# A hybrid decoder layer on one core: two slices of the last gated chunk's projection are multiplied between the first attention scores

## The reference

```
h = rmsnorm(x, norm_g)
proj = einsum('bsd,de->bse', h, w_in)
y_lru = rglru_group(u, z, ...)   # width-4 convolution, gated linear recurrence, times silu(z)
y_nsa = nsa_group(...)           # 8 heads: compressed + selected + window branch, gated, times silu(z)
y_fox = fox_group(...)           # 8 heads: causal softmax with cumulative log forget gates, times silu(z)
return x + einsum('bse,ed->bsd', concat([y_lru, y_nsa, y_fox]), w_out)
```

## Time and profile before

| | |
|---|---|
| median of the runs | 422.81 us (422.7, 422.81, 423.13) |
| the profiled execution: its time, its span | 422.76 us, 421.0 us |
| TensorE matmuls busy | 413.4 us, 98% of the span |
| VectorE, ScalarE, GpSimd busy | 285.8, 261.0, 62.5 us |
| DMA moved | 40.51 MB |
| first attention, score 0 to score 16 | 136.61 to 148.57 us |

### The profile page before, as it was taken

One profiled execution on the slowest core, in us unless ns is written; L12 is line 12 of the kernel. 1 busy time (PEld: TensorE's weight loads), 2 busy tenths in 40 slices (PEclk: granted clock), 3 DMA queues, 4 the chain that ended last, 5 costly groups with the idle time before them and its releaser, 6 DMA issues.

```text
span 421.0 us, 6567 instructions
## 1 busy us (share of the span) xinstructions
PE 413.4 (98%) x2234; PEld 325.3 (77%) x2234; DVE 285.8 (68%) x616; ACT 261.0 (62%) x519; POOL 62.5 (15%) x122
## 2 busy tenths in 40 slices
PE   8999999999999899999999999999899999999996
PEld 7876788779888766666677987988676688888885
DVE  4667749988998966776368756699777489422205
ACT  5846996687465887886087778771887554322200
POOL 3000000000000666564000000000466100000000
PEclk9999999999999999999999999999999999999999
DMA  8913534421313000000322323439410315732005
GB/s 281 360 63 101 162 93 120 132 67 41 101 51 102 0 1 2 2 1 2 121 82 74 101 75 118 134 95 221 100 42 2 100 60 205 271 99 67 2 0 199
DMA packets 14017, 40.51 MB, mean 96 GB/s; under 512 B 1928, under 2 KB 2184, under 8 KB 13728
## 3 DMA queue, kind: packets, MB, share of 16 engines
q1 hardware_dynamic: 13552, 39.51, 29.6%
q10 hardware_dynamic: 432, 0.58, 0.4%
HBM read 32.17 MB, written 2.10 MB: 81 GB/s over the span
## 4 chain that ended last, share of the span: by engine, by line
PE 84%; DVE 10%; issue 3%; ACT 1%; POOL 1%; POOLq 0%; DVEq 0%; ACTq 0%
PE bank L1423 12%; PE bank L1425 11%; PE bank L1424 11%; PE bank L1608 6%; PE bank L1589 6%; PE bank L1698 5%; PE bank L1697 5%; PE bank L1699 5%; PE bank L1579 4%; PE bank L1580 3%; PE bank L1498 2%; PE bank L1396 2%; PE bank L1630 2%; PE bank L1398 2%; PE bank L1397 2%
## 5 line engine op out<-in xcount | busy, mean ns | idle before, releaser
L1423 PE MATMUL bank<-xh,wh 128*128 128x512 f32 x240 | 99.6, 415 | 0.0
L1425 PE MATMUL bank<-xh,wl 128*128 128x512 f32 x240 | 93.8, 391 | 0.0
L1424 PE MATMUL bank<-xl,wh 128*128 128x512 f32 x240 | 93.7, 390 | 0.0
L1001 DVE TENSOR_TENSOR wl<-raw,wh 128x1024 fp32r<-128x1024 f32 (+1 forms) x50 | 60.0, 1205 | 36.6 <-ACT wh L612 36.4
L612 ACT ACTIVATE wh<-raw 128x1024 fp32r<-128x1024 f32 (+1 forms) x50 | 51.6, 1037 | 30.2 <-PE bank L1699 26.1
L1423 PEld LDWEIGHTS bank<-xh,wh 128*128 128x128 f32 x240 | 45.1, 188 | 14.9 <-issue 5.4
L1225 DVE CUSTOM_DVE_ANT_0 bank<-bank,mask_row 128x256 f32<-128x256 f32 (+3 forms) x96 | 46.6, 499 | 12.5 <-PE bank L1580 12.3
L1424 PEld LDWEIGHTS bank<-xl,wh 128*128 128x128 f32 x240 | 45.1, 188 | 11.3 <-issue 2.6
L1425 PEld LDWEIGHTS bank<-xh,wl 128*128 128x128 f32 x240 | 45.0, 188 | 9.7
L589 POOL TENSOR_SCALAR probs<-probs,rcp,gates 128x384 f32<-128x384 f32 (+3 forms) x44 | 26.5, 613 | 136.0 <-DVE rcp L1245 135.9
L1697 PE MATMUL bank<-wh,yh 128*128 128x512 f32 x96 | 37.3, 389 | 0.0
(11 more groups left out here) (246 smaller groups left out, 769.0 us busy)
## 6 DMA issues: line engine op xcount, KB each, us to landing
raw<-in_w_in SPq DMA_DIRECT2D x35, 512.0 KB, 3.4
raw<-in_w_out SPq DMA_DIRECT2D x12, 512.0 KB, 3.4
x_raw<-in_xT SPq DMA_DIRECT2D x8, 256.0 KB, 6.2
x_res<-in_x_tok SPq DMA_DIRECT2D x1, 2048.0 KB, 9.8
out_y<-y_out SPq DMA_DIRECT2D x8, 256.0 KB, 2.2
raw<-in_w_in SPq DMA_DIRECT2D x3, 384.0 KB, 3.3
cmp_w_sb<-in_cmp_w SPq DMA_DIRECT2D x1, 1024.0 KB, 5.2
kh_fox<-kh_fox SPq DMA_DIRECT2D x8, 128.0 KB, 2.3
```

Source lines behind the costliest of these rows:

```text
L1001: dve.tensor_tensor(wl[:, c % HL, cols], raw[:, c % RAW, cols], wh[:, c % HL, cols].bitcast(F32), ALU.subtract).then_inc(wl_ready, 1)
L1423: pe.matmul(dst, hi, xh[:, k, :], start=(k == 0), stop=False)
L1424: pe.matmul(dst, hi, xl[:, k, :], start=False, stop=False)
L1425: mm = pe.matmul(dst, lo, xh[:, k, :], start=False, stop=(k == KT - 1))
```

## The change

Of the chunk `zl` 3, TensorE multiplies only the first six slices (`KEPT`) in the old place. The fourth tile's transpose of the compressed branch and the scores 0 and 1 follow; slice 6 goes behind score 1, and slice 7 behind score 2. The chunk's sum no longer grows in bank 0 but in `OUT[1]` (bank 3), so that score 3 needn't wait for it. The last value product of the compressed branch, which writes the same bank, moves from step 4 to step 5 and waits for the evacuation.

On VectorE, `gated_chunk(3)` keeps the probabilities alone. The evacuation of `zl` 3 goes behind the maximum of step 3 (counted from 0), and the multiplications `zl_gate(2)` and `lru_output(2)` behind the maximum of step 12. No instruction is added or dropped, and no DMA is touched.

```diff
+KEPT = KT - 2
         def proj_bank(unit):
+            if unit + 1 in (proj_units(NSA_END),):
+                return OUT[1]
@@ gated_chunk(t), VectorE
-                if t == 3:
-                    zl_gate(2)
-                    lru_output(2)
-                evac(AT["zl", t])
+                if t < 3:
+                    evac(AT["zl", t])
@@ attention, VectorE, behind the maximum of step s
+                    if s == 3:
+                        evac(NSA_END - 1)
+                    if s == 12:
+                        zl_gate(2)
+                        lru_output(2)
@@ TensorE
-            def project(c):
+            def project(c, slices=range(KT)):
-                wait_bank(pe, unit)
+                if slices[0] == 0:
+                    wait_bank(pe, unit)
+                if c == NSA_END - 1:
+                    pe.wait_ge(cmp_o_read, NT - 2)
-                for k in range(KT):
+                for k in slices:
-                mm.then_inc(proj_done, 1)
+                if slices[-1] == KT - 1:
+                    mm.then_inc(proj_done, 1)
@@ cmp_values(t)
+                if t == NT - 1:
+                    pe.wait_ge(proj_read, proj_units(NSA_END))
@@ unit_scores(u)
-                if u in (3, NSA_UNITS + 3):
-                    pe.wait_ge(proj_read, proj_units(NSA_END if u == 3 else FOX_END))
+                if u == NSA_UNITS + 3:
+                    pe.wait_ge(proj_read, proj_units(FOX_END))
@@ attention, TensorE
                     if inside(s) is not None:
                         unit_scores(s)
-                    if s == 4:
+                    if s in (1, 2):
+                        project(NSA_END - 1, (KEPT + s - 1,))
+                    if s == 5:
                         cmp_values(NT - 1)
@@ the run of chunks, TensorE
-                project(c)
+                project(c, range(KEPT if c == NSA_END - 1 else KT))
```

More of the change, by code:

```diff
@@ L1411, in project @@
                     return
-                pe.wait_ge(wl_ready, c + 1)
-                for k in range(KT):
+                if slices[0] == 0:
+                    pe.wait_ge(wl_ready, c + 1)
+                for k in slices:
                     if k == KT // 2 and c == AT["kc", 0]:
```

## The result

The changed kernel takes 424.12 us as the median of 6 runs (423.47 to 424.83); the kernel before, measured beside it, 422.65 us (422.17 to 423.13). The ratio is 1.0034, with a 95% interval of 1.0024 to 1.0044: slower by 0.34%, 1.47 us by the medians. The forecast was 423.9 us and slower.

The account below looks back on a forecast made before the run. TensorE was taken to bound the running loop, latency its first 15 steps. Terms -0.1 (head), +0.94 (multiplies at step 12) and +0.28 (GpSimd meeting) sum to +1.1 us, giving 423.9 us, range 422.7 to 424.6.

Parts of the forecast that it names:

- the head: First steps of the first attention, up to score 6: removed wait of 0.72 us, less new waits and switches; -0.1, bounds -0.2 to 0.
- Where it is lost, and that it is never won back: First attention, step 12 on: one TensorE stall, not two, nothing recovered later because the steady period has no idle TensorE time.
- The mechanism at transpose 10: At step 12 the two moved multiplies delay VectorE's copy of probabilities 8, for which transpose 10 waits; GpSimd's scaling decides nothing.
- The stall's size: Transpose 10: +0.94 us (0.80 to 0.94) from the multiplies, plus 0.28 (0 to 0.35) from meeting GpSimd.
- By these rows the multiply is held until scaling 9 ends, 0.28: Step 12: the first multiply, with two SBUF inputs, waits for GpSimd's running scaling; 0.28 us, at most 0.35.
- The start of the value product 0.05 behind the evacuation: Compressed branch's last value product: evacuation ends at 139.05, product starts at 139.10 instead of 138.85, new wait 0.25 us.
- It takes 0.82: Compressed branch's last value product occupies TensorE for 0.82 us; transpose 0 and score 6 follow, at 140.05.
- Why score 4 waited before: Score 4 waits 0.72 us for exponential 0, late because VectorE does two multiplies and the evacuation before maximum 0.
- the free port: Step 12: no delay from GpSimd's scaling 9 beside the multiply; time 423.4 to 423.6 us, chance 0.16.
- Hidden multiplies: Step 12: VectorE has slack or TensorE is late at transpose 10 anyway; 422.7 us, chance 0.10.
- the faster case: VectorE's head start pays, transpose 3 is the only new wait, multiplies at step 12 hidden; 421.9 us, chance 0.07.
- a second stall: After step 12 VectorE doesn't catch up and scores 17 and 18 are held too, about 0.7 more; 424.6 us, chance 0.11.

## Why the prediction was right, and where its sizes were off

The forecast was +1.1 us, of which -0.1 in the head, 0.94 and 0.28 at transpose 10. Measured from the chunk on it is +1.42: 0.13 up to score 15, 1.03 at transpose 10 and 0.24 at the first value product. That is inside the range of the time, but outside the bounds of the sum, +0.6 to +1.3.

- *Where it is lost, and that it is never won back*: right. One stall at step 15, the period behind it 7.71 us as before.
- *The mechanism at transpose 10*: right, and shown: the copy (0.15 us ahead of it) and not the scaling, by moving the multiplies behind the reciprocal; nothing hidden in VectorE's slack beyond the first part, by leaving one of them in place.
- *The stall's size*: 0.94 + 0.28 = 1.22 forecast, 1.03 measured. The copy of 8 came 1.45 later, not 1.43 + 0.28. The first multiply took 0.84 from start to start (146.14 to 146.98) where 0.72 + 0.28 were forecast; the second 0.61 (to 147.59), not 0.71. The 0.71 of the earlier trace rows has a wait in it: the evacuation behind the multiply started at 136.68, when the chunk's last matmul had just ended (136.65); with the first maximum behind it instead, in the run with the multiplies back in front, the same multiply takes 0.61 too (135.80 to 136.41). The signal from VectorE to TensorE took 0.15 where I had 0.07.
- *"By these rows the multiply is held until scaling 9 ends, 0.28"*: this term was mis-sized. Scaling 9 had 0.26 to run, and the multiply took 0.81 against 0.68, so 0.13. The paragraphs behind this list have the rows for it.
- *The head*: -0.1 forecast between -0.2 and 0, +0.12 measured, outside. The start of the value product 0.05 behind the evacuation and "It takes 0.82" failed. The 0.05 held at transpose 3 (135.35 to 135.41), but the evacuation ended at 139.16 and the value product began at 139.30, 0.14 later; it occupied TensorE for 0.97 (139.30 to 140.27), not 0.82; score 0 followed the waiting transpose by 0.20, not 0.13; and the second slice's first matmul took 0.29 (137.14 to 137.43) for 0.23. For the transpose the wait is shown to cost more than its gap: without one, in the run with one slice, the 0.20 is 0.14. For the value product it is not shown: it took 0.96 or 0.97 in every changed kernel, but there it always waits, and always stands behind score 5 and no longer behind score 4.
- *Why score 4 waited before*: given only in part. The prediction lays the late exponential 0 to both multiplies and the evacuation. The kernel before with late multiplies still waits 0.56 at score 4: what held the first maximum was the evacuation, which can't start before the chunk ends.
- *What was missing*: the 0.24 us in front of the first value product. Eight waits stand there in the code and I counted them as nothing. They are nothing where TensorE isn't stalled (0.20 with eight waits or with two).
- *The rivals*: the free port is refuted, since the two engines do lengthen each other, though the meeting cost 0.13 and not 0.28; its time of 423.4 to 423.6 was missed as well. Hidden multiplies, the faster case and a second stall did not occur. That the forecast of 423.9 lies so near to 424.12 is in part luck: the stall was put too high by 0.19, the head too low by 0.23, and 0.24 was missing.

That the multiplies cost nothing where they stood was right for a reason given only in part: VectorE was waiting for the chunk there anyway, not only for the attention.

The meeting of VectorE and GpSimd. The scaling that the first multiply met in the kernel after:

```profile
145.74 0.66 POOL L592 TENSOR_SCALAR probs<-probs,rcp,gates 128x384 f32<-128x384 f32 x1
```

The rows of the prediction didn't say that the multiply is held to the scaling's end. In the earlier trace rows the scaling had 0.50 us to run when the multiply started (325.67 to 326.17), and the multiply grew by 0.35. In five meetings in which the multiply started second, it grew by what the scaling still had to run, less 0.13 to 0.16:

| where | scaling had to run, us | multiply grew by, us |
|---|---|---|
| kernel before, | 0.50 | 0.35 |
| multiplies at step 18, the second | 0.39 | 0.24 |
| behind the reciprocal, the second | 0.29 | 0.13 |
| kernel after, the first | 0.26 | 0.13 |
| behind the reciprocal, the first | 0.20 | 0.05 |

Less the 0.15 that the earlier trace rows already showed, the 0.28 becomes 0.13. The Trainium skill ("SBUF — State Buffer", Who interferes with whom) calls the ports that VectorE and GpSimd share an exclusive lock; that the second fully blocks it says of VectorE's two-port modes, and of an instruction with two SBUF inputs that it contends. These traces agree with a block here too, apart from the 0.15 or so, for which they show no reason.

## What to carry to other kernels

Work that is off the critical path has no price of its own; its price is what waits behind it in its engine's list. The same two instructions of VectorE cost nothing in front of the loop of the kernel before, 1.27 us at step 12 and 0.14 at step 18, where the engine stood waiting for a long product. So look for the place where the engine's own next instruction waits, and read how far the instructions behind it are ahead of their users.

Filling a gap of 0.72 us won nothing here, since it brought the transpose ahead of its data, and the filler shared a bank with work that then waited for it: two new waits for one. It was not the idea that failed but its places. With the multiplies out of the way and the evacuation in front of maximum 3 the same two slices won 0.25 us; with one slice, and the evacuation behind maximum 2, it was 0.45, as the first wait was gone and most of the second. These gains are read from stretches of the traces; the medians don't tell them from nothing.

Where rows show one engine lengthening another, read how much of the first instruction was left when the second started, and not only how much longer the second got. And look at both conditions of a wait: at step 18 the scaling was the one that had visibly grown, yet the copy was what the transpose waited for.

## What the runs showed of the hardware that was not expected

Waits that are long met aren't free on TensorE: eight of them ahead of a matmul cost 0.21 us more than two when TensorE has just come out of a stall (0.44 and 0.23), and nothing when it has not (0.20 either way). The length of the stall hardly matters: with one multiply it was 0.31, and the value product still came after 0.48.

A multiply of VectorE with two inputs in SBUF and a scaling of GpSimd lengthen each other by their order. The one that starts first keeps its length: scaling 9 took 0.66 in the kernel after, the first multiply of step 18 took 0.67, each with the other starting inside it. The second grows by nearly all that the first has left: the multiply by 0.05 to 0.35 for 0.20 to 0.50 left, always 0.13 to 0.16 less, the 128 wide scalings behind the reciprocal by 0.42 and 0.43 for 0.54 left.
